# Input and output projections of a decoder layer as plain fp32 products instead of three products of high and low parts

## The reference, cut to what matters

```python
mod = (c_act @ w_ada[l] + b_ada[l])[:, None, :]            # 2048 x 12288
sh1, sc1, g1, sh2, sc2, g2 = jnp.split(mod, 6, axis=-1)
h = rmsnorm(x, norm1_g[l]) * (1.0 + sc1) + sh1
proj = h @ w_in[l]                                         # 2048 x 3904
sq, sk, sv, cq, ckv, kr = jnp.split(proj, IN_SPLITS, axis=-1)
...
mixed = jnp.concatenate([rmsnorm(sb_out, out_norm_sba_g[l]),
                         rmsnorm(mla_out, out_norm_mla_g[l])], axis=-1) @ w_o[l]
x = x + g1 * mixed
h2 = rmsnorm(x, norm2_g[l]) * (1.0 + sc2) + sh2
x = x + g2 * peer_ffn(h2, w_peer_q[l], peer_keys1[l], peer_keys2[l], peer_u[l], peer_v[l])
```

## Time and profile before

| | us |
|---|---|
| median of 3 runs | 1753.91 |
| lowest and highest | 1749.77, 1756.27 |
| the profiled execution | 1751.18 |
| its span | 1749.4 |

### The profile page before, as it was taken

How to read it: one execution, slowest core, us unless ns; L and a number is a source line. 1 busy time by engine, 2 the same in 40 slices (tenths; PEclk the granted TensorE clock), 3 DMA queues, 4 the chain that set the end, 5 groups by cost and what they waited for, 6 DMA issues and landing times.

```text
span 1749.4 us, 20157 instructions
## 1 busy us (share of the span) xinstructions
PE 1478.3 (85%) x7320; PEld 980.5 (56%) x7320; DVE 1206.5 (69%) x2134; ACT 542.8 (31%) x1589; POOL 690.7 (39%) x626
## 2 busy tenths in 40 slices
PE   2979999989999998898999757656689899988874
PEld 2558987878788875666676434324333343333331
DVE  5877886879889988898454467768654555445463
ACT  3003442764311247343210146537421010101132
POOL 1000011000122354556676466555654454445461
PEclk9889999999999999999999876667789999998987
DMA  9999997849969679999999899998989999999996
GB/s 337 386 385 407 402 354 308 303 167 370 380 233 359 225 293 379 377 368 397 390 402 396 325 388 379 378 350 319 394 338 406 366 402 400 362 417 389 416 381 249
DMA packets 149806, 624.46 MB, mean 357 GB/s; under 512 B 33994, under 2 KB 38272, under 8 KB 86528
## 3 DMA queue, kind: packets, MB, share of 16 engines
q0 software_dynamic: 82976, 427.52, 62.6%
q1 hardware_dynamic: 66732, 195.67, 29.1%
HBM read 797.54 MB, written 2.10 MB: 457 GB/s over the span
## 4 chain that ended last, share of the span: by engine, by line
PE 31%; DMA 30%; DVE 24%; issue 6%; POOL 5%; ACT 3%; DVEq 1%; SPq 1%; POOLq 0%; ACTq 0%
DMA u_rows<-in_peer_u,expert 23%; DVE u_rows L2033 12%; PE ps L1167 6%; PE ps L1069 5%; PE ps L457 4%; PE ps L912 4%; DVE first_acc L486 3%; DMA v_rows<-in_peer_v,expert_rows 3%; POOL v_rows L801 3%; PE ps L906 2%; PE ps L1219 2%; PE ps L1134 2%; DMA ada_first<-in_w_ada 2%; PE ps L1204 2%; DMA u_rows<-in_peer_v,expert_rows 1%
## 5 line engine op out<-in xcount | busy, mean ns | idle before, releaser
L2033 DVE SCALAR_TENSOR_TENSOR u_rows<-u_rows,h 128x1024 f32<-128x1024 f32 (+1 forms) x416 | 595.3, 1469 | 377.9 <-DMA u_rows<-in_peer_u,expert 374.3
L801 POOL DMA_INDIRECT u_rows<-in_peer_u,expert x256 | 320.6, 1253 | 364.5 <-DVE u_rows L2033 289.5
L801 POOL DMA_INDIRECT v_rows<-in_peer_v,expert_rows x199 | 264.1, 1327 | 162.3 <-PE ps L1167 108.5
L1167 PE MATMUL ps<-v_rows,diag 128*32 128x512 f32 x1592 | 259.4, 693 | 65.1 <-DMA v_rows<-in_peer_v,expert_rows 35.6
L1219 PE MATMUL ps<-dense_rows,dense_weight 128*128 128x512 f32 x640 | 290.6, 612 | 14.9 <-DVE dense_sums L2112 8.2
L457 PE MATMUL ps<-h2T,dense_rows 128*128 128x256 f32 x1280 | 284.0, 383 | 4.2 <-ACT dense_weight L1565 4.1
L457 PEld LDWEIGHTS ps<-h2T,dense_rows 128*128 128x128 f32 x1280 | 243.4, 191 | 52.6 <-issue 17.9
L1219 PEld LDWEIGHTS ps<-dense_rows,dense_weight 128*128 128x128 f32 x640 | 123.1, 196 | 181.9 <-issue 174.9
L1167 PEld LDWEIGHTS ps<-v_rows,diag 128*32 128x32 f32 x1592 | 64.9, 125 | 182.5 <-issue 182.0
L308 POOL DMA_DIRECT2D ada_late<-in_w_ada x61 | 32.4, 531 | 303.7 <-DVE ada_acc L322 260.8
L1204 PE MATMUL ps<-high_hot,low_hot 128*128 128x40 f32 x512 | 82.1, 332 | 78.7 <-issue 54.0
(11 more groups left out here) (308 smaller groups left out, 1874.1 us busy)
## 6 DMA issues: line engine op xcount, KB each, us to landing
ada_late<-in_w_ada POOLq DMA_DIRECT2D x61, 1024.0 KB, 7.8
dense_rows<-in_dense_u SPq DMA_DIRECT2D x40, 1024.0 KB, 8.9
dense_rows<-in_dense_v SPq DMA_DIRECT2D x40, 1024.0 KB, 9.0
ada_first<-in_w_ada SPq DMA_DIRECT2D x64, 512.0 KB, 11.6
ring<-in_w_in SPq DMA_DIRECT2D x10, 2048.0 KB, 23.8
ring<-in_w_o SPq DMA_DIRECT2D x8, 2048.0 KB, 16.8
ring<-in_w_peer_q SPq DMA_DIRECT2D x8, 2048.0 KB, 13.8
opened<-in_w_in SPq DMA_DIRECT2D x8, 1024.0 KB, 13.0
```

The costliest lines, as they stand in the source:

```text
L801: nc.gpsimd.indirect_dma_start(buf[:, :], None, table, bass.IndirectOffsetOnAxis(ap=places, axis=0), bounds_check=last_sparse, oob_is_err= ...
L1167: ins = nc.tensor.matmul(ps[rows, k, :], diag[n % len(diag)][:, :], v_slot(n)[0][:, 512 * k:512 * k + 512], start=first, stop=last)
L2033: ins = nc.vector.scalar_tensor_tensor(out=u_rows[b][:, lo:hi], in0=u_rows[b][:, lo:hi], scalar=1.0, in1=h2[:, q // H, lo:hi], op0=ALU.mul ...
```

## The change

The class `Pair`, the tables and buffers of high and low parts, `h_parted` and `mixed_low` go. The five items of the input projection and the four of the output projection are multiplied in plain fp32, straight from the ring, channel by channel. The angles move from piece 0 of the opening to piece 1 (after its fourth step), their sine to after the first ScalarE part of `hT`. VectorE takes the adaLN steps 32 to 63 in one run, with only the small latent work between. The last two `squares` of attention move into the first two pairs of the output projection. A ring half is free for its next load after channel 7 of its item (input) or after the first group of heads (output).

```diff
-                for m in range(PAIRS):
-                    w = Pair(name, PAIRS * n + m, m, win_high, width)
-                    if n == 0:
-                        pe.wait_ge(h_low, m + 1)
-                    pe.wait_ge(in_low, w.c + 1)
-                    for part, mine in ((w.high, (hT_high, hT_low)), (w.low, (hT_high,))):
...
+                w = chunks(name)
+                for ch in range(KC):
+                    if ch % KH == 0:
+                        loaded(pe, name, ch // KH)
+                    last = ch == KC - 1
+                    if name[0] == "v":
+                        for t in range(TT):
+                            ins = nc.tensor.matmul(banks[t][:, 0:width], hT[:, ch, P * t:P * t + P], w[:, ch, 0:width],
+                                                   start=(ch == 0), stop=last)
...
+                    if ch == KH - 1:
+                        ins.then_inc(in_half_read, 1)
+                    if n == 2 and ch == 13:
                         ada_cols(2)
...
-            for k in range(JOBS + 6):
+            for k in range(JOBS + 4):
                 for stage, j in steps(k, (0, scores), (6, squares), (4, values), (2, middle)):
                     stage(j)
...
+                def product(h, t):
+                    ins = nc.tensor.matmul(banks[t], mix[:, h, P * t:P * t + P], w[:, h, :],
+                                           start=(h % H == 0), stop=(h % H == H - 1))
...
+                    if n == 0 and m < 2:
+                        squares(JOBS - 2 + m)
...
             for j in range(4):
                 gained(j)
                 move_h(2 * j)
-                if j:
-                    opened_read_through(dve, j - 1, 2)
-                    h_parted(j - 1)
                 if j < 3:
                     for kc in range(KC):
                         first_step(j + 1, kc)
+                        if j == 0 and kc == 3:
+                            trig_args()
                 else:
                     opened_read_through(dve, 3, 0)
-                    ada_sums(32, 34)
...
-                    Pair(name, c, m, win_high, width).make_low(dve, in_high, in_low)
...
+            ada_sums(32, 37)
+            latent_var()
+            ada_sums(37, 39)
+            for t in range(TT):
+                latent_rope(t)
...
+            ada_sums(39, 44)
+            latent_rstd()
+            ada_sums(44, 48)
+            ada_finish(2)
+            ada_sums(48, 64)
```

More of the change, by code:

```diff
@@ L423, in group, with chunks @@
         return loaded(eng, name)[:, 0:kc * width].rearrange("p (kc n) -> p kc n", kc=kc)
[L425 to L432, removed]
[L433 to L452 removed]
+    def chunks(name):
+        return ring[item[name][0]][:, :].rearrange("p (kc n) -> p kc n", kc=KC)
     def contract(half, lhs, rhs, kc):
@@ L511, in build @@
     ADA_IN, ADA_OUT = 71, 86
-    ada_after = {c: (37 + (c - 4) * 11 // 18, 37 + (c - 3) * 11 // 18) for c in range(4, 22)}
-    ada_after.update({c: (48 + (c - 25) * 11 // 15, 48 + (c - 24) * 11 // 15) for c in range(25, 40)})
     JOBS = 2 * H
@@ L1059, in _ @@
                     if m % (PAIRS // 2) == 0:
+                        g = m // (PAIRS // 2)
                         banks = [take(pe, f"w{n}_{g}_{t}") for t in range(TT)]
+                        loaded(pe, f"w_o{n}", g)
+                    pair = (2 * m, 2 * m + 1)
                     if n == 0:
-                        pe.wait_ge(mix_low, 2 * m + 2)
-                    pe.wait_ge(w_low, w.c + 1)
-                    products = [(part, k, mixed) for part, mine in ((w.high, (mix_high_part, mix_low_part)), (w.low, (mix_high_part,)))
-                                for k in range(2) for mixed in mine]
@@ L1067, in product @@
-                    def product(part, k, mixed, t):
-                        h = 2 * m + k
-                        ins = nc.tensor.matmul(banks[t], mixed[:, h, P * t:P * t + P], w.of(part, k),
-                                               start=h % H == 0 and part is w.high and mixed is mix_high_part,
-                                               stop=h % H == H - 1 and part is w.low)
-                        if h % H == H - 1 and part is w.low:
-                            fill(ins, f"w{n}_{g}_{t}")
-                        return ins
@@ L1076, in _ @@
-                    if w.c == 4 * PAIRS - 1:
+                        for h in pair:
+                            copied(pe, f"o{2 * h if h < H else 2 * (h - H) + 1}")
+                    if n == 3 and m == PAIRS - 1:
                         for t in range(TT):
-                            for p in products:
-                                product(*p, t)
+                            for h in pair:
+                                product(h, t)
                     else:
-                        for p in products:
+                        for h in pair:
@@ L1653, in _ @@
             nc.vector.reciprocal(st[:, 2:4], st[:, 2:4]).then_inc(row_rstd, 1)
[L1654 removed]
+            for kc in range(7, KC):
                 first_step(0, kc)
[L1657 to L1662 removed]
```

205 lines of the change are left out of this document (57 added, 148 removed).

## The result

The changed kernel takes 1797.64 us (median of 4 runs, 1793.51 to 1802.01) against 1755.09 us for the kernel before (median of 4): a ratio of 1.0249, 95% interval 1.0215 to 1.0283, or +42.5 us. The forecast was +42 and 1794 us.

A forecast was written before the change was run, and what follows sets the result against it. TensorE's product time was taken to bound both projections. Input products +22.6, ring +3, output products +19.9 and an earlier output start -3.4 made +42 us on 1751.2 profiled, 1793; forecast 1794 us, range 1784 to 1804.

The forecast's parts named there:

- The price of a product: In both projections, a plain fp32 instruction costs 0.216 us with 256 columns, 0.429 us with 512; two make a product.
- The rival with cheap products: In both projections, instructions take only 0.108 and 0.215 us, giving 1669 us, not slower; chance 0.03.
- Input projection, +22.6: Plain products of q, k and v take 137.8 us against 115.2 us now: +22.6 us.
- the ring +3: TensorE's wait for ring loads in the input projection, at `k0`'s second half, about 191 us: +3 us, range 0 to 8.
- After that ... the ring has the engines alone: Input projection: with the third adaLN part summed, VectorE waits for `ada_cols(2)` until about 230 us; the ring has DMA alone.
- I take 0: Lower granted clock behind `ada_cols(2)` in the input projection: 0 to +3 us possible, taken as 0.
- Output projection, +19.9 - 3.4: Plain products take 109.9 us against 90.0, +19.9 us; starting without the wait for low parts gives -3.4 us.
- The angles, 0: Moving the angles from piece 0 to piece 1 of the opening changes the time by 0, ends 0 and -4.3 us.
- Sum: Whole kernel: 22.6 + 3 + 19.9 - 3.4 = +42 us; profiled 1793 us, median 2.7 us above; 1794 us taken.
- The starved ring: Input projection: ring wait of 8 us, plus 2.7 and 3 us of low clock: +53, 1804 us; chance 0.17.
- The opening gives something: VectorE's 4.3 us in piece 0 and low parts count, the ring never waits: +35, 1786 us; chance 0.12.
- No effect: Whole kernel: the time stays within 0.5% of before; chance 0.02.
- Everything behind shifted as a block: After the output projection, all stages come later together, with the experts' stage as long as now.

The follow-up runs named there:

- `sq_back`: The changed kernel with the squares of the last two attention jobs back ahead of the output projection: 1794.68 us, ratio 1.0236 to the kernel before.
- `before_spread`: The kernel before with only the one-column products of `ada_cols(2)`, `ada_cols(4)` and `ada_cols(5)` given out two columns at a time: 1754.96 us, ratio 1.0007.
- `best`: The kernel before with the angles moved, the last squares inside the output projection and its first two pairs as plain products: 1750.75 us, ratio 0.9982.

## Why the prediction was right, step by step

- **The price of a product** held to the third digit: 0.216 us (13.83 / 64) and 0.429 us (54.95 / 128). Rows of the same form, elsewhere in the trace, were enough. The rival with cheap products falls by these rows.
- **Input projection, +22.6 and the ring +3.** From the opening's end to the last v product it took 144.9 us instead of 119.4, +25.5: 22.6 of instructions, 1.4 for the ring, 1.9 for the clock, and 0.4 less that I can't place. The ring's wait was real and small, 0 to 1.4 us in the six traces with plain input products and untouched loads, so the term of +3 was too large, and the named place was wrong: not the second half of `k0` at 191 us but the first of `k1` at 203. The fourth half was close to being late: it landed at 188.6 us, 10.5 us later than before, and was needed at 189.0. The ring's 0.134 MB/us lay between the two bounds. The step that failed is "After that ... the ring has the engines alone": VectorE's adaLN steps ran until 193.7 us and the loads that they release were in flight until 203.2, long enough to hold back the fifth half, which I had taken for safe. That VectorE then stands before `ada_finish(2)` was right (38.55 us of waiting for L325).
- **The clock.** "I take 0" was the term that failed: 1.9 us behind `ada_cols(2)`, and about 3 us behind `ada_cols(4)` (96 instructions in 44.25 us, 41.2 by their price), which the prediction did not name, since the clock had stayed at 1.00 there. One trace in which the clock did not fall was no evidence for the next kernel.
- **Output projection, +19.9 - 3.4.** The products took 113.7 us by the group of L1011 against 109.9, most of the difference being that clock. The start came as told: no idle, no slow first products, 4.6 us of squares and waiting gone and the squares back inside. `sq_back` shows that the wait for the split parts was what counted. Alone this projection cost 17.9 us against 16.5 predicted.
- **The angles, 0**: 1797.61 against 1797.64 us, and a piece 1 that ends at the same time. An effect of 1 or 2 us would not have been seen.
- **Sum.** The terms erred by -1.6 (ring), +4.9 (two clocks) and about -1.3 (the opening, which ended that much sooner in the profiled execution): the path up to `w_pq` grew by 43.9 instead of 42 us. The medians say +42.5. That the total came so close is in part luck, since the clock that was left out is offset by a ring wait that was shorter than its term and an opening that ended sooner. The forecast's time also stands a little below its own sum: 1793 and the 2.7 us of the median make 1796, not 1794.
- **The starved ring** falls, since the wait was 1.4 and not 8 us, though the fall of the clock behind `ada_cols(2)`, which it counted at 3 us, did come, at 1.9. **The opening gives something** falls as well: the ring did wait, and the opening's 1.3 us are inside the spread of its end. **No effect** is excluded by the interval.
- **Everything behind shifted as a block** held at the fourth u step, +43.6 us; the length of the rest cannot be read to better than some 5 us from single executions.

## What to carry to other kernels

Where the bounding engine is full over a stage, price the new instruction by rows of the same form elsewhere in the trace: the two prices held here to the third digit, and what the sum had wrong was the clock and the ring. A load that must land in time is held back by what another queue has in flight: here one adaLN load less in flight brought it 27 us sooner, though the time of the kernel did not show it. A saving on that engine is only worth what the next meeting point lets through: look for the one signal that another engine's queue waits for (here the last adaLN column, for the fourth gather) and move nothing past it. Splitting work at the start of a stage can be covered by doing the first pieces whole: the third pair began 4.2 us sooner so, without idle time.

## What the runs showed of the hardware

The granted clock of TensorE fell to its lower level, 1.2 GHz, for some 3 to 7 us, right behind a closed piece of 32 one-column instructions (3.5 to 4.5 us long) or in the last part of it, although TensorE had been busy all the time: at `ada_cols(2)` in the kernel before, at parts 2 and 4 in the changed kernel, at part 3 in `before_spread`. It does not do so each time: behind `ada_cols(4)` at 421 us the kernel before kept 1.00 and `best`, 4 us sooner, had 0.50. What decides between the two no run here shows. With the same instructions given out four at a time between full products, no trace of five kernels shows it in the places that were spread. The Trainium skill's page TensorE: Matmul & The Clock Gate, section "Why this matters for your kernels", names idle gaps between bursts of matmuls as what lowers the clock in mid-kernel; the rows here show it fall without any gap. Each time costs 2 to 3 us, and all other small edits to such a kernel are read through it.
